# A two-layer hybrid encoder trunk on one core: attention groups written out in full, queries turned two heads at a time in float32, outputs left feature by token

## The chip, the cores and the metric

The kernel runs on one core of a Trainium2 chip. The metric is the device time of one launch in microseconds (us); the median of three runs of the kernel before is 2032.96 us (2030.56 to 2033.18).

## The reference

Two requests (512 and 256 tokens, 768 in all, width 1024) go through the same two layers. Each layer has a gated linear attention branch (A), which the change leaves alone, and a grouped-query attention branch (B): 16 query heads of 64 channels, 4 key and value heads, so four query heads share one key head.

```python
def layer(x, ...):
    h = rmsnorm(x, norm_g)
    proj = h @ w_in
    qa, ka, va, gfl, gbl, za, qb, kb, vb, zb, ma, mb = jnp.split(proj, split_points(), axis=-1)
    ya = gla_branch(qa, ka, va, gfl, gbl, za, ...)
    yb = attn_branch(qb, kb, vb, zb, q_norm_g, k_norm_g, w_branch_b)
    merged = jax.nn.sigmoid(ma) * ya + jax.nn.sigmoid(mb) * yb
    return x + merged @ w_out

def attn_branch(qb, kb, vb, zb, q_norm_g, k_norm_g, w_branch_b):
    q, k = rotary(rmsnorm(qb)), rotary(rmsnorm(kb))      # per head of 64
    p = softmax(q @ k.T * 64 ** -0.5)                    # inside each request
    return ((p @ v) * jax.nn.silu(zb)) @ w_branch_b
```

## The kernel before

**Arithmetic.** TensorE works on rounded float32 values (`fp32r`). A float32 product is made of three matmuls: every operand is split into a high part (rounded) and a low part (the rest), and high x high, high x low and low x high are summed in PSUM. ScalarE (ACT) rounds each weight block to `w_hi` (line 934), GpSimd (POOL) makes the rest `w_lo` (line 1369), four blocks in a ring.

**Order of a layer.** Projections, four heads of branch A, rotary positions, then the attention stage: a hardware loop over the four key heads, `attention_group`. After it come four products of the branch outputs with `w_branch_a` and `w_branch_b` (`gemm_tokens`, two halves of 512 columns each) and the output projection. The order of the work on each engine is written out by hand, and semaphores tie the engines together.

**Inside an attention group** there are 20 units: 4 heads x 5 units (four tiles of 128 queries of the long request, and one unit for both tiles of the short one). For unit n TensorE (PE) turns the exponentials (`turn_p`, line 781), makes the scores of unit n + 2 (lines 769, 770), for some units the products with the values (`values`, lines 796, 797), and then some tiles of a *background* product: 96 tiles per group of the projection columns that are still missing, three matmuls each (lines 582 to 584). `ATT_TILES` says how many tiles follow each unit, `ATT_FIRST` how many come before unit 0. VectorE (DVE) takes the row maxima of unit n + 2 (line 1783), makes the low part of the turned exponentials (`lower_part`, line 1789) and adds the two parts of the outputs (line 1797). ACT takes the exponentials of unit n + 1 (line 1120), makes their turned high part (line 1130) and copies the low part of the outputs (line 1138). DVE and ACT work strictly in the order written.

**Layout of queries and keys.** For each head POOL stages a tile of 64 high and 64 low query channels (`q_st`, lines 1429 and 1432), PE turns the six token tiles (line 746), DVE copies them to `q_hl` (line 1766). The keys are staged and turned twice, once high (stacked twice) and once low. The next head's queries are turned in units 1 and 2 of the head before, four tiles and then two.

**Layout of outputs.** An output comes out of `values` feature by token. Lines 1797 and 803 to 808 put it into `o_t`, turn it back to token by feature on PE (12 tiles a group), and DVE multiplies by the inverse of the softmax sum into `q`. After the loop `q` is multiplied by silu(zb) (line 1899), turned again (line 666), and split: ACT copies the high part out of PSUM (line 997), DVE makes the low part from PSUM and that high part (line 1542).

Of the kernel before, what the change touches and what calls it, by code (L numbers as in the profile page):

```python
# [40 lines left out]
P = 128  # L41
# [55 lines left out]
def start_steps(block, first, done, blocks):  # L97
# [6 lines left out]
GLA_FIRST, ATT_FIRST = KT * NT, 20  # L104
# [5 lines left out]
ATT_TAIL = 12  # L110
ATT_TILES = (3, 3, 3, 3, 2, 2, 3, 3, 4, 2, 3, 4, 4, 4, 3, 4, 4, 3, 4, 3)
ATT_DONE = [ATT_FIRST + sum(ATT_TILES[:n + 1]) for n in range(GROUP * UNITS)]
assert ATT_DONE[-1] == BG_TILES - ATT_TAIL and KT * NT in ATT_DONE
ATT_PIECE = 9
assert [ATT_DONE[ATT_PIECE + i] for i in (-1, 0)] == [KT * NT - 2, KT * NT]
PAIR_END = (1, 3, 4)
ATT_START = start_steps(0, ATT_FIRST, ATT_DONE, BG_BLOCKS)
# [35 lines left out]
    "tensor attention group": {  # L153
        "w_lo_done": 16, "bg_free": 6, "k_staged": 2, "q_staged": 4, "k_stack": 2, "q_stack": 8,
        "exp_done": 20, "v_ready": 1, "o_drained": 4, "pt_lo_ready": 20, "o_summed": 12},
# [6 lines left out]
    "scalar attention group": {  # L162
        "w_slot0": 64, "w_used": 16, "w_slot1": 64, "w_slot2": 64, "w_slot3": 64, "stored": 32, "bg_free": 6,
        "neg_max": 20, "pr_turned": 20, "pv_done": 12, "o_summed": 12, "bg_done": 4},
# [4 lines left out]
    "gpsimd attention group": {  # L169
        "w_hi_done": 16, "pool_chain": 5, "group_free": 2, "q_turned": 8},  # L170
# [7 lines left out]
    "vector attention group": {  # L178
        "dve_chain": 2, "k_staged": 2, "k_turned": 2, "q_turned": 8, "score": 20, "pt_hi_ready": 20,
        "o_low_ready": 12, "o_turned": 4},  # L180
# [52 lines left out]
class Semaphores:  # L233


    def __init__(self, nc):
# [67 lines left out]
        self.ob_ready = sem("ob_ready")  # L304
        self.merged_ready = sem("merged_ready")
# [26 lines left out]
        self.o_turned = sem("o_turned")  # L332
        self.o_drained = sem("o_drained")
# [3 lines left out]
def trunk(nc, x_prompt, x_sample, norm_g, w_in, w_gate_f, b_gate_f, w_gate_b, b_gate_b, gla_norm_g,  # L337
# [19 lines left out]
    def rows_of(a, start, n):  # L357
# [15 lines left out]
    mb = sb("mb", [P, NT, D], R_M)  # L373
# [4 lines left out]
    o_lo = sb("o_lo", [P, KT, TOK], R_O + KT * ROW, F32R)  # L378

    b_turned = [(sb(f"b_hi{i}", [P, KT // 2, TOK], at, F32R), sb(f"b_lo{i}", [P, KT // 2, TOK], at + KT // 2 * ROW, F32R))  # L380
                for i, at in enumerate((R_ACT + KT * ROW, R_ACT))]

    g_row = sb("g_row", [P, D], R_G)
    hn = sb("hn", [P, NH, D], R_V)
# [1572 lines left out]
```

## Time and profile before

| | |
|---|---|
| median of three runs | 2032.96 us |
| the profiled execution | 2033.65 us |
| its span (first to last instruction) | 2031.8 us |
| TensorE busy, share of the span | 1961.1 us, 97% |
| VectorE, ScalarE, GpSimd busy | 983.1, 919.8, 733.1 us |
| granted TensorE clock, mean | 0.992 |
| attention stage of layer 1 | 507.1 to 789.3 us |
| attention stage of layer 2 | 1509.3 to 1791.5 us |

The profile is of one execution. Busy time of TensorE is modelled from pipelined matmuls, each shown longer than the distance to the next, so the distance between starts is what a matmul costs. The clock column gives the share of full speed (2.4 GHz) that was granted. "Idle before" a row names the instruction on another engine that ended the idle time.

### The profile page before, as it was taken

The page shows a single profiled execution, that of the slowest core. Times are in us where ns is not written, and L with a number is a line of the kernel's source. Part 1 is how long each engine was busy: PE and PEld are TensorE (multiplying, and loading weights), DVE is VectorE, ACT ScalarE, POOL GpSimd, SP SyncE. Part 2 cuts the span into 40 slices and gives each one's busy share as a digit, 9 for nine tenths or more (in the row PEclk, how much of TensorE's full clock was granted, in tenths as well). Part 3 has the DMA queues.
Part 4 walks back from the last instruction along what each step waited for, and adds up shares of the span by engine and source line. Part 5 has one row for each costly group of instructions (what it writes and reads, how often), then busy time and mean ns, then how long its engine had stood idle before and what let it go on. Part 6 is the DMA issues. An engine that isn't in the chain of part 4 may idle for free.

```text
span 2031.8 us, 37140 instructions
## 1 busy us (share of the span) xinstructions
PE 1961.1 (97%) x13184; PEld 1811.8 (89%) x13184; DVE 983.1 (48%) x1397; ACT 919.8 (45%) x1816; POOL 733.1 (36%) x744
## 2 busy tenths in 40 slices
PE   6999999999999998999999999999999999989997
PEld 6989999999999997878799899999999999978786
DVE  4113555669655653333240245556886555633224
ACT  4223555432656664423441334554336666643233
POOL 3433213258333231323553322221772332223244
PEclk9999999999999999999999999999999999989999
DMA  5322122522111114232342121225221111152324
GB/s 168 84 55 61 63 70 60 167 81 63 45 47 62 41 62 155 89 124 68 122 107 68 46 74 55 67 71 164 78 55 42 62 46 59 52 181 68 114 88 140
DMA packets 122926, 168.96 MB, mean 83 GB/s; under 512 B 15696, under 2 KB 89296, under 8 KB 122832
## 3 DMA queue, kind: packets, MB, share of 16 engines
q1 hardware_dynamic: 82656, 107.52, 18.2%
q10 hardware_dynamic: 40176, 60.18, 8.7%
q8 instruction: 61, 1.00, 0.2%
q14 instruction: 33, 0.27, 0.0%
HBM read 136.19 MB, written 31.46 MB: 83 GB/s over the span
## 4 chain that ended last, share of the span: by engine, by line
PE 87%; DVE 5%; ACT 3%; issue 2%; ACTq 1%; DMA 1%; POOL 0%; DVEq 0%; SPq 0%
PE ps L582 12%; PE ps L583 11%; PE ps L584 11%; PE ps L542 10%; PE ps L544 10%; PE ps L543 10%; PE ps L725 5%; PE ps L740 3%; PE ps L781 3%; PE ps L666 2%; PE ps L796 2%; PE ps L746 2%; PE ps L797 2%; PE ps L769 1%; PE ps L770 1%
## 5 line engine op out<-in xcount | busy, mean ns | idle before, releaser
L1369 POOL TENSOR_TENSOR w_lo<-w_raw,w_hi 128x256 fp32r<-128x256 f32 (+1 forms) x560 | 583.2, 1048 | 1227.0 <-ACT w_hi L934 1225.3
L582 PE MATMUL ps<-w_hi,act_hi 128*128 128x256 f32 x2112 | 610.0, 289 | 6.8 <-ACT stg L949 4.6
L584 PE MATMUL ps<-w_hi,act_lo 128*128 128x256 f32 x2112 | 597.2, 283 | 0.0
L583 PE MATMUL ps<-w_lo,act_hi 128*128 128x256 f32 x2112 | 597.0, 283 | 0.0
L934 ACT ACTIVATE w_hi<-w_raw 128x256 fp32r<-128x256 f32 (+1 forms) x560 | 276.4, 502 | 506.5 <-PE ps L544 294.7
L582 PEld LDWEIGHTS ps<-w_hi,act_hi 128*128 128x128 f32 x2112 | 403.6, 191 | 12.9 <-issue 4.8
L583 PEld LDWEIGHTS ps<-w_lo,act_hi 128*128 128x128 f32 x2112 | 404.0, 191 | 2.6
L584 PEld LDWEIGHTS ps<-w_hi,act_lo 128*128 128x128 f32 x2112 | 403.7, 191 | 0.0
L542 PE MATMUL ps<-w_hi,o_hi 128*128 128x512 f32 x384 | 157.4, 410 | 8.1 <-DVE o_lo L1542 5.7
L544 PE MATMUL ps<-w_hi,o_lo 128*128 128x512 f32 x384 | 152.2, 396 | 0.0
L543 PE MATMUL ps<-w_lo,o_hi 128*128 128x512 f32 x384 | 151.9, 396 | 0.0
L1783 DVE TENSOR_REDUCE st<-ps 128x1 f32<-128x512 f32 (+1 forms) x160 | 109.3, 687 | 85.9 <-PE ps L770 85.9
L1120 ACT ACTIVATE pr<-ps,st 128x512 f32<-128x512 f32 (+1 forms) x192 | 117.2, 612 | 49.5 <-DVE st L1783 47.1
L1051 ACT ACTIVATE scaled<-scaled 128x768 f32<-128x768 f32 x64 | 53.3, 833 | 162.6 <-DVE scaled L1643 161.7
L1789 DVE TENSOR_TENSOR pt_lo<-ps,pt_hi 128x512 fp32r<-128x512 f32 x128 | 88.0, 687 | 45.3 <-ACT pt_hi L1130 42.9
L1130 ACT ACTIVATE pt_hi<-ps 128x512 fp32r<-128x512 f32 x128 | 76.6, 599 | 67.0 <-PE ps L797 52.4
L1659 DVE COPY_PREDICATED amat<-mask,ps 128x768 f32<-128x768 uint8 x56 | 58.0, 1035 | 99.1 <-issue 79.3
L725 PE MATMUL ps<-scaled 128*128 128x128 f32 x768 | 102.3, 283 | 0.0
L781 PE MATMUL ps<-ident,pr 128*128 128x128 f32 x640 | 96.3, 273 | 3.6 <-ACTq L1122 3.6
L542 PEld LDWEIGHTS ps<-w_hi,o_hi 128*128 128x128 f32 x384 | 73.3, 191 | 27.7 <-DVE o_lo L1542 6.3
L725 PEld LDWEIGHTS ps<-scaled 128*128 128x128 f32 x768 | 96.9, 192 | 0.3
L544 PEld LDWEIGHTS ps<-w_hi,o_lo 128*128 128x128 f32 x384 | 73.4, 191 | 16.1
(178 smaller groups left out, 3565.0 us busy)
## 6 DMA issues: line engine op xcount, KB each, us to landing
w_raw<-in_w_in SPq DMA_DIRECT2D x352, 128.0 KB, 2.1
proj<-stg ACTq DMA_DIRECT2D x36, 768.0 KB, 3.4
w_raw<-in_w_in SPq DMA_DIRECT2D x80, 256.0 KB, 2.7
w_raw<-in_w_out SPq DMA_DIRECT2D x64, 256.0 KB, 2.5
w_raw<-in_w_branch_a SPq DMA_DIRECT2D x32, 256.0 KB, 2.6
w_raw<-in_w_branch_b SPq DMA_DIRECT2D x32, 256.0 KB, 2.5
q<-proj ACTq DMA_DIRECT2D x8, 768.0 KB, 4.7
zb<-proj ACTq DMA_DIRECT2D x8, 768.0 KB, 9.6
```

The costliest lines, as they stand in the source:

```text
L542: mm(out, s_hi, m_hi, start=first, stop=False)
L543: mm(out, s_hi, m_lo, start=False, stop=False)
L544: return mm(out, s_lo, m_hi, start=False, stop=last)
L582: mm(out, act_hi[:, k, tok], w_hi[:, k % RING, 0:BGW], start=(k == 0 and t % 2 == 0), stop=False, skip_group_check=True)
L583: mm(out, act_hi[:, k, tok], w_lo[:, k % RING, 0:BGW], start=False, stop=False, skip_group_check=True)
L584: last = mm(out, act_lo[:, k, tok], w_hi[:, k % RING, 0:BGW], start=False, stop=(k == KT - 1), skip_group_check=True)
L725: last = mm(ps[:, j * P:(j + 1) * P], lhs, rhs, start=True, stop=True)
L781: last = nc.tensor.transpose(bank(pt_bank(n))[:, place * P:(place + 1) * P], pr[:, n % 2, j * P:(j + 1) * P], ident[:])
L934: A(w_hi[:, slot, 0:width], w_raw[:, slot, 0:width], ACT.Copy).then_inc(s.w_hi_done, 1)
L1120: last = A(pr[:, n % 2, i * w:(i + 1) * w], ps[:, n % 2 * HALF + i * w:n % 2 * HALF + (i + 1) * w], ACT.Exp, bias=nmax(n, i), accum_out=de ...
L1369: G.tensor_tensor(w_lo[:, slot, 0:width], w_raw[:, slot, 0:width], w_hi[:, slot, 0:width].bitcast(F32), ALU.subtract).then_inc(s.w_lo_done, 1)
L1783: V.tensor_reduce(out, view_ps(n % 2 * HALF, (HALF // k, k), (1, HALF // k)), AX.X, ALU.max, negate=True).then_inc(s.neg_max, 1)
```

## The change

1. The hardware loop over the four groups is replaced by four written-out groups with their own `ATT_FIRST`, `ATT_TILES` and `ATT_TAIL`.
2. Queries are no longer staged on POOL. PE turns the plain float32 `q`, two heads in one 128-wide tile (12 tiles a group). ACT copies the high parts of both heads out of PSUM, 64 rows at a time, and DVE makes the low parts into the other 64 rows. The first pair of a group is turned in the last unit of the group before; the second pair in units 3, 6 and 8, two tiles each.
3. Keys are staged once by POOL (plain float32, twice side by side), turned once (6 tiles a group); ACT makes `k_hh` and DVE `k_ll` from the same PSUM tile.
4. Outputs stay feature by token: line 1797's addition writes into `q` itself; nothing is turned back. The inverse softmax sums go into silu(zb). That gate is turned instead of the gated output, and DVE multiplies it (from PSUM) into `q`; ACT then makes the high part from `q`, and DVE the low part from `q` and that high part, both in SBUF.

```diff
-ATT_TILES = (3, 3, 3, 3, 2, 2, 3, 3, 4, 2, 3, 4, 4, 4, 3, 4, 4, 3, 4, 3)
-ATT_PIECE = 9
+ATT_FIRST, ATT_TAIL = (24, 6, 6, 6), (16, 16, 16, 12)
+ATT_TILES = ((3, 3, 3, 5, 2, 2, 4, 2, 5, 3, 2, 3, 2, 3, 2, 3, 2, 3, 2, 2),) + 2 * (
+    (3, 4, 3, 6, 3, 3, 6, 3, 5, 2, 2, 2, 4, 4, 4, 4, 4, 4, 4, 4),) + (
+    (3, 4, 3, 6, 3, 3, 6, 3, 5, 2, 2, 2, 4, 5, 4, 5, 4, 5, 4, 5),)
+Q_SLOT = 0, 1, 2, 0
+Q_PARTS = {3: (0, 1), 6: (2, 3), 8: (4, 5)}
...
 # TensorE
+            def turn_keys():
+                pe.wait_ge(s.k_staged, at("k_staged"))
+                for t in range(NT):
+                    last = nc.tensor.transpose(ps[:, t * P:(t + 1) * P], view(k_st, t * P, (1, P)), ident[:])
+                last.then_inc(s.k_turned, 1)
...
                 def turn_p(n):
                     pe.wait_ge(s.exp_done, at("exp_done"))
                     pe.wait_ge(s.pt_lo_ready, at.peek("pt_lo_ready", -1))
-                    if n % UNITS in (2, 3) and n < (GROUP - 1) * UNITS:
+                    if n - 1 in Q_PARTS:
                         pe.wait_ge(s.q_stack, at("q_stack"))
...
                 for n in range(total):
                     turn_p(n)
-                    if n + 2 < total and n % UNITS != 1:
+                    if n in Q_PARTS:
+                        pe.wait_ge(s.pt_lo_ready, at.peek("pt_lo_ready", 0))
+                        turn_queries(g, 1, Q_PARTS[n], pt_bank(n + 1))
+                    if n + 2 < total:
                         scores(n + 2)
-                    if n % UNITS in (1, 2) and h < GROUP:
+                    if n == total - 1 and g + 1 < KVH:
+                        turn_keys()
                         pe.wait_ge(s.pt_lo_ready, at.peek("pt_lo_ready", 0))
-                        (q_turn_first if n % UNITS == 1 else q_turn_second)(pt_bank(n + 1))
-                    if n + 2 < total and n % UNITS == 1:
-                        scores(n + 2)
+                        turn_queries(g + 1, 0, range(4), pt_bank(n + 1))
                     if n > 0 and (n - 1) % UNITS in PAIR_END:
                         values(n - 1)
-                    if n == 2 * UNITS + 1:
-                        turn_out(range(4), 3)
-                    if n == 2 * UNITS + 3:
-                        turn_out(range(4, NT), 3)
...
+                background(0, 6)
+                turn_keys()
+                turn_queries(0, 0, range(4), pt_bank(0))
+                turn_queries(0, 0, range(4, NT), pt_bank(1))
+                background(6, 18)
+                for g in range(KVH):
+                    attention_group(g)
...
 # ScalarE
+            def high_queries(pair, tiles, b):
+                act.wait_ge(s.q_turned, at("q_turned"))
+                n = len(tiles) * P
+                for i in range(2):
+                    rows = slice(i * DH, (i + 1) * DH)
+                    last = A(q_hl[rows, Q_SLOT[2 * pair + i], tiles[0] * P:tiles[0] * P + n], ps[rows, b * HALF:b * HALF + n], ACT.Copy)
+                last.then_inc(s.q_high, 1)
...
                     if n + 1 < total:
                         exp_scores(n + 1)
                     copy_pt(n)
+                    if n in Q_PARTS:
+                        high_queries(1, Q_PARTS[n], pt_bank(n + 1))
...
+                    if n == total - 1 and g + 1 < KVH:
+                        high_keys()
+                        high_queries(0, range(4), pt_bank(n + 1))
...
 # VectorE
+            def low_queries(pair, tiles, b):
+                dve.wait_ge(s.q_high, at("q_high"))
+                n = len(tiles) * P
+                for i in range(2):
+                    of, to = slice(i * DH, (i + 1) * DH), slice((1 - i) * DH, (2 - i) * DH)
+                    slot, col = Q_SLOT[2 * pair + i], slice(tiles[0] * P, tiles[0] * P + n)
+                    last = V.tensor_tensor(q_hl[to, slot, col], ps[of, b * HALF:b * HALF + n], q_hl[of, slot, col].bitcast(F32), ALU.subtract)
+                last.then_inc(s.q_stack, 1)
...
+                    if n + 2 < total:
+                        row_max(n + 2)
+                    lower_part(n)
+                    if n in Q_PARTS:
+                        low_queries(1, Q_PARTS[n], pt_bank(n + 1))
...
+            def gated(half):
+                for t in range(NT + 1):
+                    if t < NT:
+                        dve.wait_ge(s.turned, at("turned"))
+                        some = q[:, t, half * HALF:(half + 1) * HALF]
+                        V.tensor_tensor(some, bank(6 + t % 2), some, ALU.mult).then_inc(s.b_gated, 1)
+                    if t > 0:
+                        dve.wait_ge(s.turn_hi, at("turn_hi"))
+                        V.tensor_tensor(view(b_lo, ...), view(q, ...), b_hi[half][...].bitcast(F32), ALU.subtract).then_inc(s.turn_free, 1)
```

## Rows read from the trace of the kernel before

**Rows 1.** The page: busy time by engine, and shares of the chain that ended last.

```profile
PE 1961.1 (97%) x13184; PEld 1811.8 (89%) x13184; DVE 983.1 (48%) x1397; ACT 919.8 (45%) x1816; POOL 733.1 (36%) x744
...
PE 87%; DVE 5%; ACT 3%; issue 2%; ACTq 1%; DMA 1%; POOL 0%; DVEq 0%; SPq 0%
```

**Rows 2.** Stretches (length, busy us per engine, clock, DMA share, GB/s): group 2; stage.

```profile
577.30:647.60 70.30, 68.78 (x548) 65.87 (x546) 40.46 (x69) 43.91 (x106) 21.71 (x27) 1.00 0.17 52
507.10:789.30 282.20, 275.10 (x2176) 263.28 (x2176) 164.81 (x281) 176.40 (x418) 88.22 (x104) 1.00 0.17 51
```

**Rows 3.** Groups by form, 494 to 800 us: the turns of layer 1.

```profile
L746 PE MATMUL ps<-ident,q_st 128*128 128x128 f32 x96 | 16.3, 278 | 1.2 <-DVE pt_lo L1789 0.7
...
L746 PE MATMUL ps<-ident,o_t 128*128 128x128 f32 x48 | 7.2, 272 | 0.0
...
L746 PE MATMUL ps<-ident,k_st 128*128 128x128 f32 x48 | 6.7, 275 | 0.0
```

**Rows 4.** Timeline of TensorE, third group (start, length, what): six turns.

```profile
651.98 0.82 PE L746 MATMUL ps<-ident,k_st 128*128 128x128 f32 x6
652.56 0.36 PE L582 MATMUL ps<-w_hi,act_hi 128*128 128x256 f32 x1
652.76 0.28 PE L583 MATMUL ps<-w_lo,act_hi 128*128 128x256 f32 x1
```

**Rows 5.** Timeline of TensorE, third group: places where it stood.

```profile
657.86 0.28 PE L584 MATMUL ps<-w_hi,act_lo 128*128 128x256 f32 x1
658.58 0.66 PE L781 MATMUL ps<-ident,pr 128*128 128x128 f32 x4 [0.44 <-ACTq L1122]
...
660.60 0.60 PE L781 MATMUL ps<-ident,pr 128*128 128x128 f32 x4
661.32 0.65 PE L746 MATMUL ps<-ident,q_st 128*128 128x128 f32 x4
661.73 0.48 PE L769 MATMUL ps<-k_hh,q_hl 128*128 128x512 f32 x1
...
690.68 0.38 PE L746 MATMUL ps<-ident,q_st 128*128 128x128 f32 x2
691.48 0.36 PE L796 MATMUL ps<-pt_hi,v_hl 128*128 128x256 f32 x1 [0.41 <-DVE q L1808]
...
709.42 0.60 PE L781 MATMUL ps<-ident,pr 128*128 128x128 f32 x4
710.38 0.36 PE L796 MATMUL ps<-pt_hi,v_hl 128*128 128x256 f32 x1 [0.35 <-DVE pt_lo L1789]
```

**Rows 6.** Timeline of DVE and ACT, unit 8 of the third group (it starts at 678.79).

```profile
678.54 0.69 DVE L1789 TENSOR_TENSOR pt_lo<-ps,pt_hi 128x512 fp32r<-128x512 f32 x1 [0.56 <-ACT pt_hi L1130]
679.27 0.43 DVE L1797 TENSOR_TENSOR o_t<-ps,o_low 64x256 f32<-64x256 f32 x1
...
679.76 0.20 ACT L1120 ACTIVATION_READ_ACCUMULATOR pr<-ps,st 128x1 f32 x1
680.06 0.60 ACT L1130 ACTIVATE pt_hi<-ps 128x512 fp32r<-128x512 f32 x1
```

**Rows 7.** Timeline of DVE and POOL at the start of the attention stage, layer 1.

```profile
508.72 1.76 DVE L1744 TENSOR_TENSOR va<-va,stg 128x1536 f32<-128x1536 f32 x1 [0.42 <-DVE va L1736]
...
508.95 1.90 POOL L1429 CAST q_st<-q 128x384 fp32r x1 [3.43 <-DVEq L464]
...
513.38 0.82 POOL L1440 CAST v_hl<-kv 128x768 fp32r x1
```

**Rows 8.** Timeline of TensorE, then DVE, behind the last group of layer 1.

```profile
787.50 0.82 PE L746 MATMUL ps<-ident,o_t 128*128 128x128 f32 x6
789.33 1.09 PE L666 MATMUL ps<-ident,va 128*128 128x128 f32 x8 [1.00 <-DVE q L1808]
...
790.65 1.29 DVE L1542 TENSOR_TENSOR o_lo<-ps,o_hi 128x512 fp32r<-128x512 f32 x2 [1.38 <-ACT o_hi L997]
```

**Rows 9.** Timeline of DVE: an addition with both inputs in SBUF.

```profile
909.32 1.26 DVE L1709 TENSOR_TENSOR merged<-merged,mb 128x512 f32<-128x512 f32 x1
```

More of the change, by code:

```diff
@@ L403, in trunk @@
     k_ll = sb("k_ll", [P, TOK], R_O + 5 * ROW, F32R)
-    q_hl = sb("q_hl", [P, 2, TOK], R_O + 6 * ROW, F32R)
-    q_st = sb("q_st", [P, NT, 2, DH], R_O + 8 * ROW, F32R)
-    o_t = sb("o_t", [P, TOK], R_O + 9 * ROW)
-    k_st = sb("k_st", [P, 2, NT, 2, DH], R_O + 10 * ROW, F32R)
+    q_hl = sb("q_hl", [P, 3, TOK], R_O + 6 * ROW, F32R)
+    k_st = sb("k_st", [P, NT, 2, DH], R_O + 9 * ROW)
     pr = sb("pr", [P, 2, HALF], R_O + 12 * ROW)
@@ L845, in attention_group @@
-                turn_out(range(4), 3)
-                turn_out(range(4, NT), 4)
+                if g + 1 < KVH:
+                    turn_queries(g + 1, 0, range(4, NT), pt_bank(total + 1))
+                background(done[-1] + 6, BG_TILES, ends=True)
             pe.sem_inc(s.w_used, RING)
@@ L998, in turn_hi, with gated_hi @@
                   ps[:, (base + m % 2) * HALF:(base + 1 + m % 2) * HALF].rearrange("p (a b) -> p a b", a=4), ACT.Copy).then_inc(s.turn_hi, 1)
+            def gated_hi(half, t):
+                act.wait_ge(s.b_gated, at("b_gated"))
+                at.skip("turned", 1)
+                A(b_hi[half][:, :, t * P:(t + 1) * P], view(q, t * D + half * HALF, (P, 4), (1, P)), ACT.Copy).then_inc(s.turn_hi, 1)
             def skip_banks(n):
@@ L1145, in splits_at @@
                     for i in range(BG_BLOCKS):
-                        if (-2 if i < 3 else ATT_START[i]) == n:
-                            split(i, BGW if i + SKEW < BG_BLOCKS else HALF)
+                        if ATT_START[g][i] == n and (g > 0 or i > 2):
+                            split(i, BGW if g + 1 < KVH or i + SKEW < BG_BLOCKS else HALF)
                             splits_done += 1
@@ L1161, in piece @@
                         store_sums(g * 2 + J_MA + half)
-                A(k_st[:, 0, :, :, :], view(kv, g * DH, (HALF, NT), (0, 2), (1, DH)), ACT.Copy).then_inc(s.k_staged, 1)
-                splits_at(-2)
+                if g == 0:
+                    splits_done = 1
+                    for i in (1, 2):
+                        split(i, BGW)
+                        splits_done += 1
                 total = GROUP * UNITS
@@ L1265, in _ @@
                 phase_end(act, at, s.act_phase)
-                with at.repeat(KVH, "attention group") as g:
+                split(0, BGW)
+                high_keys()
+                high_queries(0, range(4), pt_bank(0))
+                high_queries(0, range(4, NT), pt_bank(1))
+                for g in range(KVH):
                     attention_group(g)
@@ L1489, in _ @@
                 phase_ends()
-                with at.repeat(KVH, "attention group") as g:
+                stage_keys(0)
+                for g in range(KVH):
                     attention_group(g)
+                at.skip("k_turned", 1)
                 with at.repeat(4, "groups"):
@@ L1887, in _ @@
                 dve.sem_inc(s.passed, 1)
-                with at.repeat(KVH, "attention group") as g:
+                low_keys()
+                low_queries(0, range(4), pt_bank(0))
+                low_queries(0, range(4, NT), pt_bank(1))
+                for g in range(KVH):
                     attention_group(g)
```

225 lines of the change are left out of this document (82 added, 143 removed).

## The prediction

> **What bounds the kernel now.** I read the page first. TensorE is busy 97% of the span and holds 87% of the chain that ended last; DVE follows with 5% [rows 1]. So an instruction taken off TensorE is worth its distance to the next one, unless a wait takes its place, and work on another engine costs nothing while TensorE has something else to do. The stretches put the attention stage of layer 1 at 282.2 us. It is four groups of some 70.3 us, TensorE has the full clock in them, and in the second group DVE is busy 40.5 us, ACT 43.9 and POOL 21.7 [rows 2]. Hence nobody but TensorE is short of time over a group, but both ACT and DVE can be late at a single place, since they work in order. The groups by form count the turns: in layer 1 TensorE turns 96 tiles of `q_st`, 48 of `o_t` and 48 of `k_st` [rows 3]. The timeline then gives prices and places.
>
> **The price of a turn.** Six key tiles start at 651.98, the next matmul at 652.56, and the one behind it 0.20 later where 0.12 is usual (the step between background matmuls): 0.58 + 0.08 = 0.66, or 0.11 us a tile [rows 4]. Four tiles behind other turns take 661.32 to 661.73, 0.10 each [rows 5]. I take 0.11 for all.
>
> **A. Turns.** Before, a layer has 96 + 48 + 48 = 192. After, keys 4 x 6 = 24, queries 4 x 12 = 48, outputs none: 72. 120 x 0.11 = 13.2 us a layer saved. The gate's 48 tiles in the branch stage replace 48 tiles of `q`, at no difference. Scores, values and the 96 background tiles of a group stay as they were.
>
> **B. Waits that go or are covered.** I read them as the distance between starts less the usual one (0.12 for a background matmul, 0.35 for the four turned tiles of a unit), in the third group:
> - before unit 0: 657.86 to 658.58 instead of 0.12, 0.60; the exponential is late, and the slow start of the next row adds some 0.06. Two background tiles stood between scores and unit 0; now six do (2.16 us), so it goes.
> - unit 1: 660.60 to 661.32, 0.37 over; units 6 and 11 have the same wait, 0.09 and 0.44 over. They stood before the other heads' query turns, for the PSUM bank. These turns go.
> - unit 12: 690.68 to 691.48, two tiles take 0.13, so 0.67; the value product waits for `heads_out`, which goes.
> - unit 19: 709.42 to 710.38, 0.61; the value product waits for the low part. In three groups the key turns (six tiles, 0.6 us) now stand there; the last group keeps it.
>
> Together 2.84 a group, 11.4 us a layer [rows 5].
>
> **C. Waits that come.** Three times a group TensorE turns two tiles of the second pair, and may start the next unit only when ACT and DVE have split them. Unit 8 of the third group shows what they do meanwhile [rows 6]. It starts at 678.79. ACT finishes the exponentials of unit 9 at 679.96 and makes the high part from 680.06 to 680.66, 1.87 after the start. Behind it now come two copies of 64 x 256 (0.38 each, as line 1138's) to 2.7. DVE takes the row maximum and the low part, ends about 2.7, then two subtractions of 64 x 256 (0.42, as line 1797's) with a small gap each: 3.65, and TensorE goes at 3.75. Its own work in between: 0.35 for the unit's turn, 0.2 for the two tiles, 0.55 for the scores, 0.36 for each background tile, and before the two tiles a bank wait: the low part of the unit before is done 1.6 after the end of its value product, against 0.36 a tile and 0.35 of turn. That gives:
> - groups 2 to 4: unit 3 (six tiles) bank 0.2, then 3.75 against 3.46, 0.35 with rounding up; unit 6 (six tiles, exponential earlier, ready at 3.6 against 3.26) 0.35; unit 8 (five tiles) bank 0.2, then 0.7. Sum 1.8 each, 5.4.
> - group 1 has fewer tiles there (5, 4, 5, and 2 before unit 8): 0.2 + 0.7, then 0.05 + 1.07, then 0.55 + 0.7 = 3.3.
> - unit 19 of the last group as before: 0.6.
> - the start of the stage. The keys are now staged by POOL alone, and TensorE wants them after six tiles, not twelve: at 507.1 + 6 x 0.36 = 509.3. POOL can't begin before 508.95, where its first copy took 1.90 us beside a DVE multiplication with both inputs in SBUF that ended at 510.48; the same kind of copy at twice the output takes 0.82 alone [rows 7]. Nearest row: the copy ends some 0.75 behind that multiplication, at 511.2. TensorE stands 1.9 us. Bounds: 0.5, if POOL isn't held up, and 2.3.
>
> Sum 5.4 + 3.3 + 0.6 + 1.9 = 11.2 us a layer, so B and C nearly cancel: 0.2 saved. The in-group part, 9.3, is my least certain number, since each wait is a difference of two times near 3.5 us. Bounds: zero, if ACT and DVE come 0.7 earlier (nothing in the rows allows more than that at units 3 and 6), and twice it, 18.6, if each is as much later.
>
> The VectorE rule on instructions with no wait between them (the Trainium skill, "VectorE: DVE Perf Modes", section "Two Vector instructions with no wait between them") speaks against the new subtractions: an instruction whose input or output starts at another group of 32 partitions than its predecessor's begins only when the predecessor has ended. Two low parts in full rows take 1.29 where one takes 0.69, an overlap of 0.09 [rows 8]; line 1797's, on 64 rows, begins at 679.27, 0.04 behind its predecessor's end at 679.23 [rows 6]. The trace agrees with the rule. Without it each pair would be 0.15 shorter, 24 pairs, and the sum would be 3.6 us lower, 2002.3.
>
> **D. Moved at no cost.** The first pair and the keys of the next group are turned in unit 19 and behind the last values. ACT and DVE need about 1 us each for the keys and 1.2 and 1.4 for four query tiles (by the rows of unit 8, scaled with the columns); counted from unit 19's start they are through with the last two tiles at 8.0 (group 1) or 8.7, and TensorE, with 18 or 20 background tiles and two value products in between, gets to the scores at 9.5 or 10.2. Cover 1.5 us. The last two tiles alone have ten background tiles (3.6 us) behind them; if all of it went, three waits of up to 2.1 us a layer. POOL loses the query staging (0.5 + 1.0 us a head), which hid nothing. ACT's table load at the head of each loop turn probably comes once a layer; it wasn't on the path.
>
> **E. End of the stage.** Before, six output turns (in A) run from 787.50, and the next turns start at 789.33, 1.0 of it idle for `heads_out` [rows 8]: 1.2 us of waiting. After, TensorE still has to wait for ACT's copies of the last background sums, until about 788.6, 1.1 us. 0.15 saved.
>
> **F. The gate.** In the branch stage a turn now passes DVE (0.69), ACT (0.60) and DVE again. The last is a subtraction with both inputs in SBUF; such an addition took up to 1.26 beside POOL [rows 9], against 0.69. DVE has 1.4 to 1.95 us of work for each turn, and turns come every 2.5 us (nine matmuls of 512 columns, 0.21 us each at 2.4 GHz, and the turn of four tiles), so the ring of two banks keeps up. Behind the last turn of a half stands at least one block of weights (4.1 us) before TensorE wants the result; the chain takes some 3.2. Cost nothing; if uncovered, the added 0.69 for each of 24 turns, 16.6 us.
>
> **The sum.** 13.2 + 0.2 + 0.15 = 13.55 us a layer, 27.1 for both. The profiled execution would go from 2033.65 to 2006.6; its span leaves 1.85 us outside, unchanged. The median lies 0.7 below that execution, hence 2032.96 - 27.1 = 2005.9.
>
> **Rivals.**
> - *The covers hold.* ACT and DVE are done before TensorE at every second-pair batch, and the 9.3 a layer is gone: 2005.9 - 18.6 = 1987.3. For it: POOL's pressure falls, and waits that compare with loop registers become constants. Against: the rows of unit 8 leave no room at units 8 and, in group 1, at 6. More likely is half of it, inside the forecast's range. 0.12.
> - *The second-pair waits are twice as large.* + 18.6: 2024.5. For it: ACT ends the exponential of unit 9 only 1.17 behind the unit's start. 0.10.
> - *The gate chain comes to the surface* (F): 2022.5. 0.05.
> - *Slower: ACT falls a step behind at the second pair.* If the two high copies at units 3, 6 and 8 stand behind one more exponential (0.88) and one more weight split (0.41), each of the 24 batches frees TensorE 1.3 us later: + 31, 2037. It decides from 1.13 us more at each batch (27.1 / 24). Against: 44 of 70 us busy on ACT, and a written order in which the copies come before the split. 0.03.
> - *The change doesn't do what it says*: written-out code that is fetched late, or turns that were never on the path. Turns are on an engine that is busy 97%, so only the former is left, and no row names such a wait. 0.02, to either side of no change.
>
> **How the numbers follow.** The forecast, waits between half and one and a half of my sum, has 0.68 and reaches from 1996 to 2016. The rivals above and below have 0.12 and 0.17, the rest 0.03. The range 1994 to 2016 leaves out some 0.2. About 0.2% (4 us) is what a measurement can tell from no change. Faster 0.95, same 0.01, slower 0.04.
>
> **What would show it.** 72 turns a layer in the attention stage at 0.11 us; a group of near 66 us instead of 70.3 (second and third); a wait of near 2 us for `k_st` at its start; waits on `q_hl` before units 4, 7 and 9, largest before unit 7 of the first group; no wait before unit 0; no new wait in the products of branch B. The prediction is wrong if those waits are absent or over a microsecond each, or if a turn of plain `q` costs other than 0.11.

## The result, and the profile after

| | before | after |
|---|---|---|
| median of the runs, us | 2032.64 | 2010.39 |
| range | 2030.56 to 2033.18 | 2009.47 to 2011.72 |
| profiled execution / its span | 2033.65 / 2031.8 | 2011.16 / 2009.4 |
| attention stage, layer 1 and 2 | 282.3, 282.3 | 270.9, 270.9 |

The ratio of the medians is 0.9893 (95% interval 0.9876 to 0.991): faster by 22.3 us, where 27.1 were forecast. The profiled execution is 22.5 shorter, and the two attention stages account for 22.8. A stage is counted here from its first background matmul (507.03 in the kernel before) to the first turn behind it.

The page of the kernel after, busy time by engine and the chain [rows 1]:

```profile
PE 1935.8 (96%) x12944; PEld 1787.6 (89%) x12944; DVE 976.4 (49%) x1375; ACT 943.4 (47%) x1890; POOL 675.9 (34%) x688
...
PE 87%; DVE 6%; ACT 3%; issue 2%; ACTq 1%; DMA 0%; POOL 0%; DVEq 0%; SPq 0%
```

TensorE issues 240 matmuls fewer (120 a layer), but its busy share falls from 97 to 96%, and DVE's share of the chain rises from 5 to 6%: more of the time is now spent waiting. The stretches, stage and second group [rows 2]:

```profile
507.54:778.42 270.88, 262.51 (x2057) 250.88 (x2057) 153.09 (x256) 187.84 (x455) 59.59 (x76) 1.00 0.18 54
578.30:645.20 66.90, 65.47 (x517) 62.75 (x516) 37.34 (x63) 46.33 (x114) 14.23 (x19) 1.00 0.18 56
```

The turns by form, layer 1 [rows 3]: 48 + 24 = 72.

```profile
L743 PE MATMUL ps<-ident,q 128*128 128x128 f32 x48 | 8.9, 283 | 0.4 <-DVE pt_lo L1786 0.3
...
L736 PE MATMUL ps<-ident,k_st 128*128 128x128 f32 x24 | 3.3, 275 | 0.0
```

The timeline of TensorE, places where it stood in group 1 (up to 545.08) and group 2 [rows 5]:

```profile
529.55 0.63 PE L768 MATMUL ps<-ident,pr 128*128 128x128 f32 x4 [0.73 <-DVE q_hl L1771]
...
537.89 0.63 PE L768 MATMUL ps<-ident,pr 128*128 128x128 f32 x4 [0.94 <-DVE q_hl L1771]
...
541.42 0.44 PE L743 MATMUL ps<-ident,q 128*128 128x128 f32 x2 [0.32 <-DVE pt_lo L1786]
...
545.08 0.39 PE L571 MATMUL ps<-w_hi,act_hi 128*128 128x256 f32 x1 [1.32 <-ACT stg L918]
...
592.48 0.63 PE L768 MATMUL ps<-ident,pr 128*128 128x128 f32 x4 [0.20 <-DVE q_hl L1771]
...
601.52 0.63 PE L768 MATMUL ps<-ident,pr 128*128 128x128 f32 x4 [0.21 <-DVE q_hl L1771]
...
608.48 0.63 PE L768 MATMUL ps<-ident,pr 128*128 128x128 f32 x4 [0.72 <-DVE q_hl L1771]
...
621.98 0.39 PE L782 MATMUL ps<-pt_hi,v_hl 128*128 128x256 f32 x1 [0.29 <-DVE pt_lo L1786]
```

The first three rows and those from 592 to 608 are the second pair's waits: before units 4 and 7 of group 1, for the PSUM bank in its unit 8 (541.42), and before units 4, 7 and 9 of group 2. Two were not foreseen: 545.08, a background tile of unit 8 in group 1 that waits for ACT's copy of the background sums, and 621.98, the value product in unit 14.

**A table of units.** A unit runs from the turn of its `pr` tiles to that of the next. I take from its length what TensorE issues in it, at the steps of the timeline (0.36 a background tile, 0.11 a turn, 0.21 a score matmul of 512 columns and 0.11 one of 256, 0.12 a value matmul); what is left is waiting, with some 0.03 of rounding. Worked out so (us waited, tiles of the unit in brackets):

| unit | after | e3 | e5 | e7 | e9 | e10 | e11 |
|---|---|---|---|---|---|---|---|
| group 2, 3 | 0.57 (6) | 0.40 (7) | 0.03 (6) | 0.40 (7) | 0.21 (6) | 0.19 (6) | 0.18 (6) |
| 6 | 0.38 (6) | 0.03 (7) | 0.03 (6) | 0.05 (7) | 0.02 (6) | 0.16 (5) | 0.15 (5) |
| 8 | 1.09 (5) | 0.35 (7) | 0.05 (5) | 0.35 (7) | 0.55 (5) | 0.19 (6) | 0.21 (6) |
| 12 | 0.15 (4) | 0.77 (6) | 0.17 (4) | 0.16 (4) | 0.16 (4) | 0.76 (5) | 0.16 (4) |
| 14 | 0.63 (4) | 0.02 (4) | 0.60 (4) | 0.04 (4) | 0.62 (4) | 0.01 (4) | 0.04 (4) |
| group 1, 3 | 1.09 (5) | 0.58 (7) | 0.05 (5) | 0.58 (7) | 0.56 (5) | 0.55 (5) | 0.21 (6) |
| 6 | 1.11 (4) | 0.21 (7) | 0.02 (4) | 0.23 (7) | 0.51 (4) | 0.51 (4) | 0.15 (5) |
| 8 | 2.15 (5) | 2.17 (8) | 1.58 (5) | 2.09 (8) | 2.17 (5) | 1.94 (4) | 0.51 (4) |
| 14 | 0.30 (2) | 0.63 (2) | 0.30 (2) | 0.62 (2) | 0.31 (2) | 0.04 (2) | 0.62 (2) |

Groups 3 and 4 are as group 2 within 0.04, but for unit 14 of group 4 (0.24 in the kernel after) and its unit 12 in e10 (0.15, with four tiles).

### The profile page after: what moved, and what is told of

Same layout as the page of the kernel before. It is cut to its first block, busy times and chain, and to the rows that moved or that the text cites. A ratio compares the mean times of both kernels' runs of the same rounds, so it can differ in the third digit from the quotient of the medians.

```text
span 2009.4 us, 34921 instructions
## 1 busy us (share of the span) xinstructions
PE 1935.8 (96%) x12944; PEld 1787.6 (89%) x12944; DVE 976.4 (49%) x1375; ACT 943.4 (47%) x1890; POOL 675.9 (34%) x688
## 3 DMA queue, kind: packets, MB, share of 16 engines
q1 hardware_dynamic: 82656, 107.52, 18.6%
## 4 chain that ended last, share of the span: by engine, by line
PE 87%; DVE 6%; ACT 3%; issue 2%; ACTq 1%; DMA 0%; POOL 0%; DVEq 0%; SPq 0%
PE ps L571 12%; PE ps L572 11%; PE ps L573 11%; PE ps L532 10%; PE ps L534 10%; PE ps L533 10%; PE ps L714 5%; PE ps L729 3%; PE ps L768 3%; PE ps L782 2%; PE ps L655 2%; PE ps L783 2%; PE ps L757 2%; PE ps L758 2%; DVE q_hl L1771 1%
## 5 line engine op out<-in xcount | busy, mean ns | idle before, releaser
L1373 POOL TENSOR_TENSOR w_lo<-w_raw,w_hi 128x256 fp32r<-128x256 f32 (+1 forms) x560 | 571.6, 1027 | 1287.5 <-ACT w_hi L903 1285.7
L1780 DVE TENSOR_REDUCE st<-ps 128x1 f32<-128x512 f32 (+1 forms) x160 | 109.8, 690 | 142.3 <-PE ps L758 141.9
L1110 ACT ACTIVATE pr<-ps,st 128x512 f32<-128x512 f32 (+1 forms) x192 | 117.0, 611 | 12.2 <-DVE st L1780 10.2
L768 PE MATMUL ps<-ident,pr 128*128 128x128 f32 x640 | 96.8, 274 | 10.2 <-DVE q_hl L1771 10.2
L714 PEld LDWEIGHTS ps<-scaled 128*128 128x128 f32 x768 | 96.9, 192 | 0.3
```

What stands on the lines that cost most here:

```text
L714: last = mm(ps[:, j * P:(j + 1) * P], lhs, rhs, start=True, stop=True)
L768: last = nc.tensor.transpose(bank(pt_bank(n))[:, place * P:(place + 1) * P], pr[:, n % 2, j * P:(j + 1) * P], ident[:])
L1110: last = A(pr[:, n % 2, i * w:(i + 1) * w], ps[:, n % 2 * HALF + i * w:n % 2 * HALF + (i + 1) * w], ACT.Exp, bias=nmax(n, i), accum_out=de ...
L1373: G.tensor_tensor(w_lo[:, slot, 0:width], w_raw[:, slot, 0:width], w_hi[:, slot, 0:width].bitcast(F32), ALU.subtract).then_inc(s.w_lo_done, 1)
L1780: V.tensor_reduce(out, view_ps(n % 2 * HALF, (HALF // k, k), (1, HALF // k)), AX.X, ALU.max, negate=True).then_inc(s.neg_max, 1)
```

## Experiments

All are compared with the kernel before on their own chip. "Stage" is the attention stage of layer 1, a row of the stretches; "end" runs from the first turn behind the stage to the first matmul of the second branch product, both layers added, by the timeline. The kernels ran on different chips; on these the kernel before took 2032.5 to 2033.9.

| kernel | median, us | ratio, 95% interval | stage | end |
|---|---|---|---|---|
| before | 2032.6 | | 282.30 | 94.3 |
| e1 written out | 2028.0 | 0.9975 (0.9966 to 0.9984) | 280.09 | 94.7 |
| e2 + outputs | 2019.6 | 0.9935 (0.9921 to 0.9949) | 274.45 | 96.6 |
| after | 2010.4 | 0.9893 (0.9876 to 0.991) | 270.88 | 94.3 |
| e3 tiles | 2005.5 | 0.9867 (0.9852 to 0.9882) | 267.52 | 94.4 |
| e4 part later | 2012.4 | 0.9899 (0.9883 to 0.9914) | 271.14 | 95.9 |
| e5 no second pair | 1987.6 | 0.9781 (0.9768 to 0.9794) | 259.35 | 97.6 |
| e6 double turns | 2022.3 | 0.995 (0.9936 to 0.9963) | 275.87 | 95.3 |
| e7 tiles, order of one copy | 2000.4 | 0.9842 (0.9829 to 0.9856) | 265.32 | 96.1 |
| e8 + short tail | 1999.7 | 0.9838 (0.9825 to 0.9851) | 264.34 | 96.9 |
| e9 queries first | 2001.6 | 0.9841 (0.9827 to 0.9854) | 265.80 | 95.1 |
| e10 e9 + tiles | 1999.8 | 0.9833 (0.982 to 0.9847) | 264.79 | 95.1 |
| e11 | 1995.1 | 0.9814 (0.98 to 0.9827) | 263.02 | 95.7 |
| e12 e11 + loads later | 1988.0 | 0.9783 (0.9769 to 0.9797) | 263.20 | 86.5 |

**e1, e2: the change in three parts.** In e1, on all four engines of the kernel before:

```diff
-with at.repeat(KVH, "attention group") as g:
+for g in range(KVH):
```

> The kernel before, with nothing changed but that the four attention groups of a layer are written out on all four engines instead of standing in a hardware loop. Theory (the gain comes from turns and waits that go, and written-out code is worth nothing): 2032.6 us as before, between 2030 and 2034; 192 turns in the attention stage of a layer, stage of layer 1 near 282 us. Rival (part of the gain of 22 us is the loop: waits against registers, table loads at each turn of the loop): 2010 to 2028, and the more of it the less is left for the turns. Rival of the other side (written-out code is fetched late): over 2036.

> The groups written out and the output part of the change alone: outputs stay feature by token in q, the gate is turned and multiplied in, no output turns and no heads_out; queries and keys are staged, turned and stacked as before, with the old numbers of background tiles. Theory (terms add): 48 turns less at 0.11 us = 5.3 us a layer, the wait for heads_out before the value product of unit 12, 0.67 in each of 4 groups = 2.7, and 0.15 at the end: 8.1 a layer, 16.3 in all, 2016.3 us; then the other part of the change (queries and keys) brought only some 6 us of the 22.3, since its 72 turns less (8.1 a layer) and its covered waits are eaten by the new waits on q_hl. Rival (the wait for heads_out only hid another, late low part or late ACT): 5.5 a layer, 2021.5. Rival (the branch stage pays for the longer gate chain, hidden in the comparison of totals): over 2025.

e1 stands at the rival's upper edge (2028): 2.2 us a layer belong to the loop alone, which my sum did not have. DVE's timeline shows the largest piece. In the kernel before, third group:

```profile
690.17 0.22 DVE L1802 RECIPROCAL st<-st 128x12 f32<-128x12 f32 x1
690.64 0.69 DVE L1808 TENSOR_TENSOR q<-ps,st 128x512 f32 x1 [0.24 <-DVE st L1802]
```

and in e1:

```profile
688.90 0.22 DVE L1791 RECIPROCAL st<-st 128x12 f32<-128x12 f32 x1
689.16 0.69 DVE L1797 TENSOR_TENSOR q<-ps,st 128x512 f32<-128x512 f32 x1
```

The gap between the two falls from 0.25 to 0.04; the wait of unit 12 falls by 0.3, those of units 1 and 11 by 0.1 each, 0.5 of the 0.55 a group. The outputs then bring 5.6 a layer in the stage. Of the 8.1 that I expected from e2 against before, 7.85 came, but 2.2 of it are the loop's, so the outputs' own part was sized too high: 48 turns give 5.3 and unit 12 another 1.2, but 0.3 comes back in the last unit of each of three groups. The median is 3.3 above the forecast, 2.3 of it lost behind the stage (the column "end"; e12 takes that up). Queries and keys bring the last 3.6. Stage lengths: 2.2 + 5.6 + 3.6 = 11.4.

**e6: what a turn costs.** `for t in 2 * list(range(NT))` in `turn_keys`, and twice the tiles in `turn_queries` for the first pair.

> The changed kernel with each turn of the keys and of the first pair made twice, into the same place: 24 + 24 turns more a layer, nothing else. Theory (turns cost 0.11 each on TensorE and the first pair and the keys are covered on ACT and DVE): 48 x 0.11 = 5.3 a layer, 10.6 in all, 2021.0 us, between 2019.5 and 2022. Rival (the added time is taken from waits that stand behind the turns): 2011 to 2017. Rival (the copies come later and uncover the first pair): over 2024.

The stage grows by 4.99 for 48 turns, 0.104 each. But unit 19 of group 1, where TensorE waits for a PSUM bank behind the key turns, waits 0.42 in the kernel after and 0.09 here, so 0.33 of the added turns filled a wait, and a turn costs (4.99 + 0.33) / 48 = 0.11. The median grows by 11.9, 9.8 of it in the two stages and 1.0 in "end". The price holds (the median is 0.3 above the range), and the first pair stays covered.

**e5: what the second pair costs.**

```diff
-Q_SLOT = 0, 1, 2, 0
-Q_PARTS = {3: (0, 1), 6: (2, 3), 8: (4, 5)}
+Q_SLOT = 0, 1, 0, 1
+Q_PARTS = {}
```

> The changed kernel without the second pair: heads 3 and 4 of a group use the queries of heads 1 and 2 (two slots, 0, 1, 0, 1), so nothing is turned, copied or subtracted at units 3, 6 and 8; the tiles per unit stay. It leaves those queries out of the computation. Theory (the second pair costs its 24 turns a layer, 2.7 us, and the waits that the unit table shows at it: 2.0 in each of groups 2 to 4, 4.3 in group 1, of which 0.3 to 1.3 belong to the background sums): 11.5 to 12.5 a layer gained, 1986 us, between 1984 and 1989. Rival (ACT and DVE are short over whole stretches, so half of the waits come back at other units): 1992 to 1998. Rival (the turns alone, the waits stay): 2005.

11.5 a layer in the stage, 22.8 by the medians: the theory's lower edge. The waits of units 3, 6 and 8 go altogether and come back nowhere. But unit 8 of group 1 keeps 1.58 without any query in it, and unit 14 its 0.6: those two do not come from the queries.

**e4: is unit 8 of group 1 a collision?** `Q_PARTS` of group 1 is `{3: (0, 1), 6: (2, 3), 11: (4, 5)}`, with 3 tiles at unit 8 and 5 at 11.

> The changed kernel with the last two query tiles of the second pair turned at unit 11 instead of unit 8 in group 1 alone (background tiles 3 at unit 8 and 5 at unit 11 instead of 5 and 3). Theory (in group 1 the two high copies of 64 x 256 stand ahead of the copy of the third pair of background sums in ACT's order, and that collision makes the 1.58 us that TensorE stands inside unit 8's background): that wait falls to 0.3 to 0.8, a wait of 0.5 to 0.9 on q_hl comes before unit 12, 0.3 to 1.0 a layer gained, 2008.4 to 2009.8 us. Rival (the copy is late because of the exponentials and the second value product, whatever the queries do): the wait inside unit 8 stays above 1.2 and the time is 2010.4 to 2012.5.

Neither holds, though the time is in the rival's range. The wait inside unit 8 fell to 0.24, which does not show a collision either: two tiles left the unit together with the queries, and e5, with no queries and all five tiles, keeps 1.58 there. And units 9, 10 and 11 now wait 0.63, 0.41 and 0.87, so that the five units 8 to 12 take 15.0 us instead of 14.6.

**e3, e7, e8: tiles moved.** e3's numbers for groups 2 and 3, and in e7 the copy's place in ACT's order in group 1 (it is left out where it stood before):

```diff
-    (3, 4, 3, 6, 3, 3, 6, 3, 5, 2, 2, 2, 4, 4, 4, 4, 4, 4, 4, 4),) + (
+    (2, 3, 3, 7, 2, 2, 7, 3, 7, 2, 2, 2, 6, 4, 4, 4, 4, 4, 3, 3),) + (
...
+                    if g == 0 and n == ATT_PIECE[g] + 1:
+                        piece(0, 2)
                     if n + 1 < total:
                         exp_scores(n + 1)
```

> The changed kernel with other numbers of background tiles per unit, the sum the same: 7, 7 and 7 (group 1: 7, 7, 8) at units 3, 6 and 8 instead of 6, 6, 5 (5, 4, 5), 6 at unit 12 of groups 2 to 4, fewer around them, and 22 instead of 24 ahead of unit 0 in group 1. Theory (each wait is a chain of fixed length on ACT and DVE less what TensorE has to do in the unit, so a tile of 0.36 us takes 0.36 off a wait): groups 2 to 4 lose the waits of 0.39, 0.39 and 0.7 of the 0.91 and the 0.55 before unit 13, some 1.7 each after small new ones, group 1 loses 0.7 + 1.0: 6.5 a layer, 13 in all, 1997.5 us. Rival (ACT and DVE are behind by their total load, and a wait covered here comes back at the next unit with few tiles): under 3 us gained, 2007 to 2013, with as much idle time under other lines. Either way the wait inside unit 8's background of group 1 stays near 1.5 us.

> The numbers of background tiles of the run before with two corrections: 4 and 6 tiles at units 12 and 13 of groups 2 to 4 instead of 6 and 4, and in group 1 the copy of the third pair of background sums stands ahead of unit 9's exponential and of the two high copies in ACT's order, where it stood behind them. Theory (the 0.6 at unit 12 is the fifth tile of the second half waiting for that copy, and the 1.3 inside unit 8 of group 1 is the same copy standing behind 2.2 us of other work on ACT): 0.6 in three groups and 1.2 in one gained against that run, 3.0 a layer, 6 in all, 1999.5 us, between 1997.5 and 2001.5. Rival (what ACT does first makes something else late: the wait for q_hl or the low part before the value products grows by as much): 2003 to 2006.

> As e7, with two tiles fewer behind the last unit of groups 1 to 3 (14 instead of 16) and two more among units 13 to 19. Theory (the first pair's chain is covered with 1.5 us to spare, so two tiles of 0.36 can go, and the few small waits of units with 2 or 3 tiles in group 1 shrink): 0.2 to 0.5 a group gained, 1997 to 1999 us. Rival (the cover behind the last unit is already used up): a wait of up to 0.7 before the scores of the next group, 2000 to 2004.

e3 gained 4.9 of the 13 expected, and both readings hold in places. At units 6 and 8 of groups 2 to 4 a tile took its 0.36 off the wait. At unit 3 it took 0.17 (0.57 to 0.40). At unit 12 I had put the fifth tile of the second half in reach of the third copy of the sums. e3's timeline:

```profile
616.98 0.39 PE L571 MATMUL ps<-w_hi,act_hi 128*128 128x256 f32 x1 [0.34 <-ACT stg L918]
```

e7 put 4 and 6 tiles at units 12 and 13, and the stage fell by 2.2; the median is in the theory's range. Its other half failed instructively: with the copy first, the wait inside unit 8 of group 1 is gone and stands one row later, before unit 9:

```profile
543.65 0.63 PE L768 MATMUL ps<-ident,pr 128*128 128x128 f32 x4 [1.36 <-DVE q_hl L1773]
```

So in group 1 ACT is short of time over units 8 and 9. In the kernel after its timeline has no gap there. Ahead of the first row ACT itself had stood 2.54 us, until the value product of unit 7, and TensorE had started unit 7 late for `q_hl` (537.89 above):

```profile
540.04 0.60 ACT L1120 ACTIVATE pt_hi<-ps 128x512 fp32r<-128x512 f32 x1 [2.54 <-PE ps L783]
540.67 0.38 ACT L1128 ACTIVATE o_low<-ps 64x256 f32<-64x256 f32 x1
541.07 1.08 ACT L918 ACTIVATE stg<-ps 128x512 f32<-128x512 f32 x2
542.04 0.48 ACT L1110 ACTIVATE pr<-ps,st 128x256 f32<-128x256 f32 x1
...
543.16 0.60 ACT L1120 ACTIVATE pt_hi<-ps 128x512 fp32r<-128x512 f32 x1
543.65 0.76 ACT L1100 ACTIVATE q_hl<-ps 64x256 fp32r<-64x256 f32 x2
544.43 0.60 ACT L918 ACTIVATE stg<-ps 128x512 f32<-128x512 f32 x1
```

e8 shortened the stage by 1.0 against e7; the medians are too near each other to show it.

**e9: the order in the two queues.** On ACT, and alike on DVE with `low_queries` and `lower_part`:

```diff
-                    copy_pt(n)
                     if n in Q_PARTS:
                         high_queries(1, Q_PARTS[n], pt_bank(n + 1))
+                    copy_pt(n)
```

> The changed kernel with its own numbers of tiles and one other order at units 3, 6 and 8: ACT makes the two high copies ahead of the copy of the turned probabilities (pt_hi), and DVE the two subtractions ahead of the lower part (pt_lo). Theory (the wait for q_hl is a chain of fixed length, and only what stands ahead of the queries in the two orders counts; the low part in front of them, 0.69 us on DVE, goes out of it): each of these waits falls by up to 0.65; groups 2 to 4: 0.36, 0.35 and 0.65, group 1: 0.65, 0.65 and nothing at unit 8, where the background sums rule: 5.3 a layer, 10.7 in all, 1999.7 us, between 1997 and 2002. Rival (ACT and DVE are behind by their load, so the later pt_lo makes the value products of units 4, 7 and 9 wait instead): 2007 to 2011. Rival (slower: the next unit's exponential is late too): over 2011.

The stage fell by 5.1, forecast 5.3; on this chip the kernel before was 1.3 slower, so the median's 2001.6 and the ratio agree with it. Units 3, 6 and 8 of group 2 lose 0.36, 0.36 and 0.54, units 3 and 6 of group 1 lose 0.53 and 0.60, and no value product waits longer. The waits of TensorE for `q_hl` in the kernel after, then in e9 (us in total, times, longest):

```profile
PE ps L768 <- DVE q_hl L1771: 10.2, 22, 0.9
```

```profile
PE ps L768 <- DVE q_hl L1771: 2.2, 10, 0.3
```

This is the one test that moves no work, so the order alone made this much of the wait: 5.1 of the 11.5 us a layer that e5 gained. Unit 8 of group 1 and the smaller rests are not touched by it.

**e10, e11: both together.** e11 adds to e9: groups 2 and 3 `(3, 4, 3, 6, 3, 3, 5, 3, 6, 2, 2, 2, 4, 6, 4, 4, 4, 5, 4, 3)`, group 1 `(3, 3, 3, 6, 2, 2, 5, 2, 4, 5, 3, 5, 2, 2, 2, 2, 2, 2, 2, 3)` with the last part at unit 11 and 22 tiles ahead; group 4 differs from 2 and 3 behind unit 14 only; 14 tiles stand behind the last unit of groups 1 to 3.

> As e9, and the tiles spread for that order: groups 2 to 4 with 5, 6 at units 6, 8 and 6 at unit 13, group 1 with 4 tiles at unit 8, so that its fifth tile of the second half comes a unit later, and 14 instead of 16 tiles behind the last unit of groups 1 to 3. Theory: against e9 the 0.6 before unit 14's value product goes in three groups (0.25 in the last), unit 8 loses 0.3 in three groups, and the 1.3 inside unit 8 of group 1 becomes 0.3: some 3.5 a layer, 1993 us, between 1990 and 1996. Rival (group 1 is bound by ACT's copies of the background sums and waits elsewhere for them, as it did with the later part): 1995 to 1998.

> As e10, with three things set by the waits found so far: unit 12 of groups 2 and 3 has 4 tiles again, so that its fifth does not meet the copy of the background sums; in group 1 the last two query tiles go to unit 11, and units 8 to 11 have 4, 5, 3 and 5 tiles, since ACT's load is what counts there; group 1 starts unit 0 after 22 tiles and has 6 and 5 at units 3 and 6. Theory: 0.6 in each of two groups, 1.3 at units 8 to 11 and 0.7 at units 3 and 6 of group 1, less up to 0.6 for short units behind: 2.0 to 3.0 a layer against e10, 1994.5 us, between 1993 and 1997. Rival (group 1 is bound by ACT over the whole stretch, whatever stands where, as the earlier run with the later part showed): 1996.5 to 1999.

e10 missed both ranges, since I repeated e3's mistake (5 tiles at unit 12 of groups 2 and 3, 0.76) and group 1 answered as in e7: 1.22 for `q_hl` before unit 9. e11 came where it was expected. Unit 12 of groups 2 and 3 loses its 0.6 each. In group 1 units 3 and 6 lose 0.7, and unit 8 loses 1.4, with more of TensorE's work over units 8 to 11 where ACT is short. But units 9 and 11 take 0.5 of that back and the shorter units 13, 14 and 17 wait 1.1 more, where up to 0.6 was expected: group 1 as a whole gains 0.7.

**e12: the loads behind the stage.**

```diff
                 for t in range(NT):
                     turn_hi(o_hi, t, t)
-                    if t < 4:
-                        fetch(zb, J_ZB + t, t * BGW, D, 1, s.zb_in)
+                for t in range(4):
+                    fetch(zb, J_ZB + t, t * BGW, D, 1, s.zb_in)
```

> As e11, and behind the attention stage ACT issues the four loads of branch B's gate (zb) after its six copies of turned tiles instead of between them. Theory (TensorE waits 3 to 4 us before the first branch product for o_lo, and ACT was late for it because each of the four DMA issues in its queue took 0.4 to 3.0 us; the length of these issues differs from kernel to kernel and is the 1 to 2 us a layer by which the time from the stage's end to that product varies): 2.5 to 4 a layer gained, 5 to 8 in all against e11, near 1988 us. Rival (the loads are then late for the gate, or the weights' splits stand behind the issues and stop the product): within 2 of e11, or slower.

7.1 us by the medians, and the column "end" 9.3 shorter than in e11; the stage of layer 1 began 1.7 later in this execution (below). ACT's timeline in the kernel after shows the loads in its queue:

```profile
781.41 0.76 ACTq L944 DMA_DIRECT2D zb<-proj  x1
782.22 0.60 ACT L966 ACTIVATE o_hi<-ps 128x512 fp32r<-128x512 f32 x1 [0.23 <-issue]
782.23 3.02 ACTq L944 DMA_DIRECT2D zb<-proj  x1
785.30 0.60 ACT L966 ACTIVATE o_hi<-ps 128x512 fp32r<-128x512 f32 x1 [2.49 <-issue]
```

TensorE's first product, in the kernel after, in e11 and in e12:

```profile
787.28 0.79 PE L532 MATMUL ps<-w_hi,o_hi 128*128 128x512 f32 x1 [3.03 <-DVE o_lo L1537]
```

```profile
778.59 0.80 PE L532 MATMUL ps<-w_hi,o_hi 128*128 128x512 f32 x1 [3.42 <-DVE o_lo L1537]
```

```profile
777.56 0.50 PE L532 MATMUL ps<-w_hi,o_hi 128*128 128x512 f32 x1 [1.41 <-DVE o_lo L1537]
```

The theory has only half of it. From the stage's end to this matmul e12 takes 2.9 us less than e11 in layer 1 and 1.9 less in layer 2, 4.8 together, where 2.5 to 4 a layer was expected. The other 4.5 come in the product behind it, whose work is the same. These are its stretches in layer 1, e11 and then e12, with the granted clock behind the fifth engine:

```profile
778.59:817.16 38.57, 38.31 (x168) 31.26 (x169) 17.02 (x15) 18.74 (x22) 14.50 (x8) 0.93 0.54 172
```

```profile
777.56:813.62 36.06, 35.80 (x169) 29.33 (x169) 16.93 (x15) 19.27 (x23) 14.82 (x8) 1.00 0.72 232
```

In e11 the clock is 0.50, the lower level of 1.2 GHz, from 774 to 784: it fell while TensorE had only a few turns between waits, and the first matmuls of 512 columns start every 0.43 us instead of every 0.23. Layer 2 is alike for the product (0.94 against 1.00, 38.1 against 36.0 us), though in e12 the clock is low for a while among the turns. In the kernels before and after the product has 0.93 to 0.96. So in these runs time lost behind the stage is paid twice, as idle time and as a slow start of the product, and the median came to the forecast partly by a term that the forecast did not have. No run changes the clock alone.

## Why the prediction was right, and where it was off

The direction, the likeliest case and the range held. The sum was 4.8 us too good: 13.55 a layer forecast, 11.4 measured in the stage. C was off in two places, by 3.4 too little in the groups and by 1.8 too much at the start; that they partly cancel is luck. Of the signs that I named, 72 turns, a group of 66.9 and the longest wait for `q_hl` before unit 7 of group 1 (0.94) came. The wait of near 2 us for `k_st` did not. And I had called waits of over a microsecond each a sign of being wrong: by the table of units the one in unit 8 is 1.09, and the three of group 1 are 1.09, 1.11 and 2.15. So the time came out better than the picture of the waits behind it.

- **A, turns.** 72 a layer, 0.11 each (e6): right.
- **B, waits that go.** All went. The loop's 0.55 a group was in those rows, and I had explained it by the output and query turns alone. Counted over the whole stage by the steps of the table of units, waits and rounding together are 15.4 us before and 17.3 after. With 12.9 new ones (below) 11.0 went, where B and E have 11.55.
- **C, waits that come: the term that was mis-sized.** Forecast 11.2, of it 9.3 in the groups. Groups 2 to 4: 1.8 forecast each, 1.95 measured (0.57, 0.38, 1.09 less rounding). Group 1: 3.3 against 4.3; the bank wait and the wait for `q_hl` of unit 8 did not add as I had them; ACT's copy of the sums stood behind both (1.32), and e5 has that wait without any query. Not in the sum at all: the value product of unit 14, 1.6 over the groups (it stays in e5, so the queries don't bring it; e7 removes it by tiles alone), unit 12 0.4, units 18 and 19 of group 1 0.5. The last group's 0.6 at unit 19 did not come. In all 12.7 instead of 9.3.
- **C, start of the stage.** 1.9 forecast, 0.1 measured. Timelines of POOL, DVE and TensorE:

```profile
509.03 0.82 POOL L1430 COPY k_st<-kv 128x768 f32<-128x768 f32 x1 [3.09 <-DVEq L454]
509.82 2.25 POOL L1373 TENSOR_TENSOR w_lo<-w_raw,w_hi 128x256 fp32r<-128x256 f32 x1
```

```profile
509.13 2.34 DVE L1739 TENSOR_TENSOR va<-va,stg 128x1536 f32<-128x1536 f32 x1 [0.41 <-DVE va L1731]
```

```profile
509.91 0.88 PE L736 MATMUL ps<-ident,k_st 128*128 128x128 f32 x6
```

POOL's copy began 0.1 ahead of the multiplication and took its 0.82; it was DVE that took 0.58 longer than before [rows 7], and POOL's next instruction took 2.25. This is below the lower bound that I gave (0.5). The Trainium skill, "SBUF — State Buffer", section "Terms", says that the loser of the two at the shared port is blocked in full. The rows agree roughly: DVE lost 0.58 of the 0.72 us in which both were under way. Which of the two loses, the runs show by the order of starts. Wherever the new staging copy meets the multiplication, POOL starts 0.1 ahead and its copy keeps 0.82; in the kernel before DVE starts 0.23 ahead and keeps 1.76 while POOL's copy takes 1.90; in e1, where both start at 508.71, DVE keeps 1.76 and POOL's copy takes 2.12.

- **The VectorE rule** (the Trainium skill, "VectorE: DVE Perf Modes", section "Two Vector instructions with no wait between them"). 32 subtractions of 64 x 256 in a layer take 0.42 each and a pair 0.86, with no overlap: as the rule has it. No run here takes the held start away, so its price was not measured. I had 0.15 a pair, where its rows give 0.09 + 0.04 = 0.13.
- **D, keys and first pair moved.** Nothing waits for them, and with two tiles fewer behind the unit (e8) neither: right. But their turns cost a wait of their own in group 1, where TensorE must wait for a bank before it turns the four tiles. The row starts 0.36 behind the turn ahead of it instead of 0.11, and e6 fills that time with turns:

```profile
568.79 0.82 PE L736 MATMUL ps<-ident,k_st 128*128 128x128 f32 x6
569.70 0.66 PE L743 MATMUL ps<-ident,q 128*128 128x128 f32 x4
```

- **E, F.** The wait for ACT's copies at the end is there: 1.1 by the starts, as forecast. The gate is turned in the second and third product, behind what "end" covers. From the first matmul of the second to the last of the fourth it is 109.8 us in both layers of both kernels: the gate chain costs nothing, as forecast.
- **The rivals.** "Covers hold" is where e9 gets a little over half the way by order alone, 10.2 of the 18.6 us. Something like "ACT falls a step behind" happened at one batch of twelve a layer, unit 8 of group 1, where copies of the background sums stand between, not one more exponential and weight split.

So the 2.15 us a layer are C, 1.7 net, and B with E, 0.5. Still open: which rows of B gave less than counted, and why the wait of unit 3 yields less than a tile per tile (e3).

## What to carry to other kernels

When a wait hangs on the end of a chain through two engines that work in order, look first at what stands ahead of it in their orders and is needed later: e9 gained 5.1 of the 11.5 us a layer that leaving out the work gained (e5), without moving a tile. Cover moved by hand (e3, e10) meets other edges, here a PSUM bank that a third engine must free; list those edges with the tile numbers before moving. Where a wait only changes its name when the order changes (e4, e7), the engine is short over a stretch, and what helped here was more of the bound engine's work in that stretch, as far as the units that gave up their tiles could spare it (e11). And where TensorE stands for microseconds, look at the granted clock behind the wait before you price it by its length (e12).

## What was not expected of the hardware

- A DMA issue holds ACT's queue for 0.4 to 3.0 us in the first layer of the kernel after (four loads of 768 KB), and the next copy starts only then. By the Trainium skill, "DMA: Bandwidth & Descriptors", section "Issuing engines are not separate DMA queues", the time to initiate a DMA is usually small beside the DMA. It was 3.02 beside 12.2 from issue to landing for that load, and 3.87 for all four in e12, so the rows bear that out only loosely.
- Behind the wait of 3.0 us (after) and 3.4 us (e11) in layer 1 the granted clock was at its lower level in the first microseconds of the next product, and in e12, behind 1.4 us, it was not. The issues and this clock together were worth 7.1 us. "End" lies between 94.3 and 97.6 in the other kernels, 17.4 to 20.9 of it the way to the first matmul and 75.2 to 77.5 the product at 0.92 to 0.96 of the clock.
- The stage of layer 1 begins at 505.9 to 506.0 in four kernels (e2, e7, e10, e11) and at 507.0 to 507.6 in the others, though nothing ahead of it was changed in the experiments. The granted clock of the profiled execution goes with it: from 20 to 27 us it is 1.00 in these four and 0.76 in all the others. ACT and DVE of e10 and e9 are in step up to 20 us and 1.6 us apart from 36 us on. So this time is in no stage length, and as nothing ahead of it differs between the kernels, it likely belongs to the execution and not to the edits. The stretches of e9 and of e10, from 20 us:

```profile
20.00:27.00 7.00, 5.49 (x22) 5.48 (x23) 2.08 (x4) 6.37 (x18) 4.78 (x5) 0.76 0.36 91
```

```profile
20.00:27.00 7.00, 5.48 (x31) 5.48 (x32) 3.08 (x8) 6.82 (x20) 4.82 (x5) 1.00 0.38 96
```

- Instructions written out instead of looped are worth 0.6 us per turn of the loop here (e1), half of it at unit 12, where DVE writes `q` at a place that the loop's index gives. That this is the reason was not shown.
